# All three gate stages of a two-block kernel: pairs 2 to 17 by seven block products for eight on contraction tiles 0 to 3, in 256 columns

## The reference, cut to what matters

```python
D_MODEL, SEQ, D_FF = 1024, 512, 2816

def swiglu(x, w_gate, w_up, w_down):                     # stage gu0
    return (jax.nn.silu(x @ w_gate) * (x @ w_up)) @ w_down

def _conv_ffn(x, w_in, conv_w, conv_b, w_out):           # stages gu1, gu2
    s = x.shape[1]
    u = x @ w_in                                         # 1024 x 5632
    up = jnp.pad(u, ((0, 0), (CONV_WIDTH_2 - 1, 0), (0, 0)))
    u = sum(conv_w[j] * up[:, j:j + s] for j in range(CONV_WIDTH_2)) + conv_b
    g, val = u[..., :D_FF_2], u[..., D_FF_2:]
    return (jax.nn.silu(g) * val) @ w_out
```

## Time and profile before

| | |
|---|---|
| median of 3 runs | 1810.29 us (1809.44 to 1810.98) |
| the profiled execution, its own time | 1813.07 us |
| its span | 1811.3 us |
| mean granted clock of TensorE | 0.993 |
| busy: PE, DVE, ACT, POOL | 97%, 42%, 44%, 57% |
| the chain that ended last: PE, DVE, ACT | 84%, 10%, 2% |

### The profile page before, as it was taken

The page is one execution under the profiler, slowest core; times in us unless marked ns, Lnnn a source line. Parts: engine busy times, 40 slices in busy tenths (PEclk is TensorE's granted clock), DMA queues, the critical chain, the costliest instruction groups (busy, mean ns, idle before and its releaser), DMA issues.

```text
span 1811.3 us, 26859 instructions
## 1 busy us (share of the span) xinstructions
PE 1765.7 (97%) x8755; PEld 1478.9 (82%) x8755; DVE 768.1 (42%) x1382; ACT 796.2 (44%) x1674; POOL 1031.5 (57%) x926
## 2 busy tenths in 40 slices
PE   8999999999999999999999999989999999999997
PEld 6879888888887888798888888877777888888887
DVE  7973000001235556553333322487875533333224
ACT  5644332322245555464444422555555644444231
POOL 7956555555562333456666665555554666666651
PEclk9999999999999999989999999999999999999999
DMA  5212333333334454323333233333332233332332
GB/s 159 87 47 82 105 93 93 95 88 109 91 95 110 124 134 119 87 68 105 93 100 96 78 111 89 82 85 85 85 83 68 73 106 102 93 97 85 105 91 98
DMA packets 327252, 171.94 MB, mean 95 GB/s; under 512 B 43458, under 2 KB 316948, under 8 KB 327188
## 3 DMA queue, kind: packets, MB, share of 16 engines
q1 hardware_dynamic: 327172, 171.12, 33.6%
q10 hardware_dynamic: 16, 0.00, 0.0%
HBM read 152.15 MB, written 2.10 MB: 85 GB/s over the span
## 4 chain that ended last, share of the span: by engine, by line
PE 84%; DVE 10%; ACT 2%; issue 1%; DMA 1%; POOL 1%; SPq 1%; DVEq 0%; ACTq 0%
PE bank L983 23%; PE bank L985 23%; PE bank L984 23%; DVE score L2266 3%; PE attended L983 2%; PE attended L984 2%; PE attended L985 2%; PE turned L1424 1%; PE attended L1440 1%; PE bank L1056 1%; PE bank L1068 1%; DVE small L2454 1%; PE bank L1069 1%; ACT pmap L1861 1%; DMA raw<-in_a_w_in 0%
## 5 line engine op out<-in xcount | busy, mean ns | idle before, releaser
L742 POOL TENSOR_TENSOR WL<-raw,WH 128x512 fp32r<-128x512 f32 (+3 forms) x656 | 776.8, 1206 | 541.5 <-ACT WH L1605 538.9
L983 PE MATMUL bank<-XL,WH 128*128 128x512 f32 x1432 | 568.7, 397 | 3.7 <-DVE work L2577 1.2
L985 PE MATMUL bank<-XH,WL 128*128 128x512 f32 x1432 | 557.5, 389 | 0.0
L984 PE MATMUL bank<-XH,WH 128*128 128x512 f32 x1432 | 557.0, 389 | 0.0
L1605 ACT ACTIVATE WH<-raw 128x512 fp32r<-128x512 f32 (+3 forms) x656 | 338.4, 566 | 295.6 <-PE bank L985 183.2
L985 PEld LDWEIGHTS bank<-XH,WL 128*128 128x128 f32 x1432 | 269.3, 188 | 56.8
L983 PEld LDWEIGHTS bank<-XL,WH 128*128 128x128 f32 x1432 | 269.9, 188 | 55.6 <-DVE work L2577 1.5
L984 PEld LDWEIGHTS bank<-XH,WH 128*128 128x128 f32 x1432 | 270.1, 189 | 50.4
L983 PE MATMUL bank<-HL,WH 128*128 128x512 f32 (+1 forms) x528 | 198.6, 376 | 0.0
L985 PE MATMUL bank<-HH,WL 128*128 128x512 f32 (+1 forms) x528 | 198.4, 376 | 0.0
L984 PE MATMUL bank<-HH,WH 128*128 128x512 f32 (+1 forms) x528 | 198.4, 376 | 0.0
(11 more groups left out here) (366 smaller groups left out, 2534.0 us busy)
## 6 DMA issues: line engine op xcount, KB each, us to landing
raw<-in_ffn_w_in SPq DMA_DIRECT2D x88, 512.0 KB, 3.6
raw<-in_w_gate SPq DMA_DIRECT2D x22, 512.0 KB, 3.6
raw<-in_w_up SPq DMA_DIRECT2D x22, 512.0 KB, 3.7
raw<-in_ffn_w_out SPq DMA_DIRECT2D x28, 384.0 KB, 3.2
raw<-in_ffn_w_out SPq DMA_DIRECT2D x28, 320.0 KB, 3.2
raw<-in_a_w_in SPq DMA_DIRECT2D x16, 512.0 KB, 3.9
raw<-in_kv_w SPq DMA_DIRECT2D x32, 256.0 KB, 2.9
raw<-in_w_in SPq DMA_DIRECT2D x12, 512.0 KB, 3.6
```

Source lines behind the costliest of these rows:

```text
L742: pool.tensor_tensor(wl, x, wh, ALU.subtract).then_inc(w_lo, 1)
L983: pe.matmul(out_, wh, xl, start=start, stop=False)
L984: pe.matmul(out_, wh, xh, start=False, stop=False)
L985: return pe.matmul(out_, wl, xh, start=False, stop=stop)
```

## The change

Pairs 0, 1 and 18 to 21 stay as they were. For the 16 pairs 2 to 17 of each gate stage ("fast" pairs) the contraction tiles 0 to 3 are seen as a two by two block problem: two blocks of contraction tiles (0 and 1, 2 and 3), the two outputs (up, gate), two halves of 256 tokens. Seven block products stand for the eight, each of 2 contraction tiles, 3 matmuls, 256 columns (6 matmuls); contraction tiles 4 to 7 are multiplied plainly, in 256 columns too (48 matmuls). The output of a pair comes together in three PSUM banks of a set (two sets alternate); four intermediate sums are kept aside by ACT (`keep`), and DVE adds them to the finished halves (`pair_sum`), which gives the two banks `bank` that the rest of the pair reads as before.

The weights of a fast pair fall in three groups: **A**, plain weights of the first four contraction tiles (high and low of 6 tiles, 768 columns; raw buffer doubled), **S**, four sums of weights (8 tiles, 1024 columns; summed by DVE, high by ACT, low by DVE), and **P**, gate's and up's contraction tiles 4 to 7 (8 tiles, 1024 columns; high by ACT, low by POOL; one raw buffer, two sets of high and low). Four sums of tokens are made once a stage by DVE, split by ACT and DVE. The step names of PE's order are r1, a, q1, r2, u, r3, q, r. `clear_sums` moves from the norm ahead of the stage to behind the last fast pair. The core of the diff:

```diff
+FAST = ("gu0", "gu1", "gu2")
+FAST_FIRST, FAST_PAIRS = 2, 16
+FAST_LAST = FAST_FIRST + FAST_PAIRS - 1
+TAIL_PAIRS = range(FAST_LAST + 1, FT)
+FAST_STEPS = ("r1", "a", "q1", "r2", "u", "r3", "q", "r")
+KEPT = (("r1", 1.0), ("q1", -1.0), ("r2", -1.0), ("r3", -1.0))
+KEPT_OF_SUM = (0, 3, 2, 1)
+SUM_AFTER = ("u", "u", "q", "r")
+SETS_FREE = 2 * len(KEPT)
...
+def gu_items(name):
+    return 2 * (FT - FAST_PAIRS) if name in FAST else 2 * FT
...
+        raw_a = [raw_fast[:, :, :], raw[:, 0, :, :]]
+        raw_p = raw[:, 1, :, :]
...
+        WA = [ring_tiles(x, 0, 6) for x in (WH, WL)]
+        WS = [ring_tiles(x, 6, 8) for x in (WH, WL)]
+        WP = [[ring_tiles(x, 14 + 8 * b, 8) for x in (WH, WL)] for b in range(2)]
+        token_sums = [x[:, FAST_LAST + 1:FT, :] for x in (HH, HL)]
+        w_sums = work[:, 0:2, :].rearrange("p a (k n) -> p (a k) n", n=P)
+        kept_tiles = [work[:, 2 + 2 * b:4 + 2 * b, :].rearrange("p a (k s) -> p (a k) s", s=HALF) for b in range(2)]
...
+        fast_sets = [(sc[0], sc[1], tb[0]), (tb[1], ob[0], ob[1])]
...
+                def load_a(n, i):
+                    b = n.slot(2)
+                    for part, w, t in ((0, up, i + up_first), (4, gate, i)):
+                        sp.dma_start(raw_a[b][:, part:part + 4, :], w[:, 0:4, bass.ds(t.n() * P, P)]).then_inc(a_landed[b], 16)
+                def load_p(n, i):
+                    for part, w, t in ((0, gate, i), (4, up, i + up_first)):
+                        sp.dma_start(raw_p[:, part:part + 4, :], w[:, 4:DT, bass.ds(t.n() * P, P)]).then_inc(p_landed, 16)
+                def load_pair(i):
+                    n = fast_pair(name, i)
+                    sp.wait_ge(a_lo, n.n(-1))
+                    sp.wait_ge(w_summed, n.n(-1))
+                    load_a(n, i)
+                    sp.wait_ge(p_lo, n.n())
+                    load_p(n, i)
+                def load_plain(g):
...
+                def of_a(i):
+                    n = fast_pair(name, i)
+                    pool.wait_ge(a_hi, n.n(1))
+                    pool.tensor_tensor(WA[1], raw_a[n.slot(2)][:, 2:DT, :], WA[0].bitcast(F32), ALU.subtract).then_inc(a_lo, 1)
+                def of_p(i):
+                    n = fast_pair(name, i)
+                    b = n.slot(2)
+                    pool.wait_ge(p_hi, n.n(1))
+                    pool.tensor_tensor(WP[b][1], raw_p, WP[b][0].bitcast(F32), ALU.subtract).then_inc(p_lo, 1)
+                def of_hid(i):
+                    j = i.slot(2)
+                    pool.wait_ge(h_hi, (i + FT * layer).n(1))
+                    pool.tensor_tensor(HL[:, at(i), :], hid[:, j:j + 1, :], HH[:, at(i), :].bitcast(F32), ALU.subtract).then_inc(h_lo[j], 1)
+                def slot(i):
+                    of_a(i + 1)
+                    of_hid(i + -1)
+                    of_p(i + 1)
...
+                def add(out_, ws, xs, opens=False, closes=False):
+                    for t, (w, x) in enumerate(zip(ws, xs)):
+                        mm = product(out_, w[0], w[1], x[0], x[1], opens and t == 0, closes and t == 1, not opens)
+                    return mm
+                def plain(out_, side, c, ks=range(4)):
+                    for k in ks:
+                        w = [x[:, 4 * side + k, :] for x in WP[b]]
+                        mm = product(out_, w[0], w[1], XH[:, 4 + k, c], XL[:, 4 + k, c], False, k == 3, True)
+                    return mm
+                r, q = running[:, 0:HALF], second[:, 0:HALF]
+                u_gate, u_up = mixed[:, low_half], mixed[:, high_half]
+                x = (XH, XL)
+                pe.wait_ge(a_lo, n.n(1))
+                pe.wait_ge(pair_sums, n.times(4).n(4 + SETS_FREE - 8))
+                if b == 1:
+                    for side in range(2):
+                        pe.wait_ge(bank_read[side], STAGES[name][1] // 2 + 2)
+                add(r, weights(WA, 2), tokens(x, 0, low_half), True, True).then_inc(fast_mm, 1)
+                add(u_up, weights(WA, 0), sums_of_tokens(3), True, True)
+                add(u_gate, weights(WA, 4), tokens(x, 2, low_half)).then_inc(fast_mm, 1)
+                pe.wait_ge(p_lo, n.n(1))
+                plain(u_gate, 0, low_half, range(2))
+                plain(u_up, 1, low_half, range(2))
+                pe.wait_ge(s_lo, n.n(1))
+                add(q, weights(WS, 0), sums_of_tokens(1), True, True).then_inc(fast_mm, 1)
+                pe.wait_ge(kept, n.times(4).n(1))
+                add(r, weights(WS, 4), sums_of_tokens(2), closes=True).then_inc(fast_mm, 1)
+                plain(u_gate, 0, low_half, range(2, 4))
+                plain(u_up, 1, low_half, range(2, 4)).then_inc(fast_mm, 1)
+                pe.wait_ge(kept, n.times(4).n(3))
+                add(r, weights(WS, 2), sums_of_tokens(0), closes=True).then_inc(fast_mm, 1)
+                add(q, weights(WS, 6), tokens(x, 2, high_half))
+                plain(q, 0, high_half).then_inc(fast_mm, 1)
+                pe.wait_ge(kept, n.times(4).n(4))
+                plain(r, 1, high_half).then_inc(fast_mm, 1)
...
+            def keep(n, k):
+                step, sign = KEPT[k]
+                b = n.slot(2)
+                act.wait_ge(fast_mm, n.times(len(FAST_STEPS)).n(after(step)))
+                act.activation(kept_tiles[b][:, k, :], fast_sets[b][1 if step[0] == "q" else 2][:, 0:HALF], ACT.Copy,
+                               scale=sign).then_inc(kept, 1)
...
+            def a_high(name, i):
+                n = fast_pair(name, i)
+                b = n.slot(2)
+                act.wait_ge(a_landed[b], n.round(2, 1) * 32)
+                if first_fast(n):
+                    act.wait_ge(item_done, STAGES[name][0] + 2)
+                else:
+                    act.wait_ge(fast_mm, n.times(len(FAST_STEPS)).n(after("a") - len(FAST_STEPS)))
...
+            def p_high(name, i):
+                act.wait_ge(p_landed, n.times(32).n(32))
+                if isinstance(i.it, int) and i.base < FAST_FIRST + 2:
+                    act.wait_ge(item_done, STAGES[name][0] + 3 + b)
+                else:
+                    act.wait_ge(fast_mm, n.times(len(FAST_STEPS)).n(-len(FAST_STEPS)))
...
+            def s_high(name, i):
+                n = fast_pair(name, i)
+                act.wait_ge(w_summed, n.n(1))
+                if not first_fast(n):
+                    act.wait_ge(fast_mm, n.times(len(FAST_STEPS)).n(after("q") - len(FAST_STEPS)))
+                act.activation(WS[0], w_sums, ACT.Copy).then_inc(s_hi, 1)
...
+            def fast_gates(name):
...
+                def slot(i):
+                    n = fast_pair(name, i)
+                    keep(n, 0)
+                    hidden(i + -1)
+                    a_high(name, i + 1)
+                    p_high(name, i + 1)
+                    for k in range(1, 4):
+                        keep(n, k)
+                    s_high(name, i + 1)
...
+            def fast_conv_hidden(name, layer):
...
+                def slot(i):
+                    n = fast_pair(name, i)
+                    keep(n, 0)
+                    linear_fast(i + -1, 1)
+                    a_high(name, i + 1)
+                    p_high(name, i + 1)
+                    silu_fast(i + -1)
+                    keep(n, 1)
+                    keep(n, 2)
+                    hidden(i + -1)
+                    keep(n, 3)
+                    s_high(name, i + 1)
...
+                with act.Fori(0, FAST_PAIRS // 2 - 1) as it:
+                    for j in range(2):
+                        i = Nth(FAST_FIRST + 1 + j, it, 2)
+                        linear_fast(i + -1, 0)
+                        slot(i)
...
+            def sums_of_weights(name, i, m):
+                n = fast_pair(name, i)
+                b = n.slot(2)
+                dve.wait_ge(a_landed[b], n.round(2, 1) * 32)
+                if first_fast(n):
+                    dve.wait_ge(x_lo, DT + half_tile(m, 1, DT - 1) + 1)
+                else:
+                    dve.wait_ge(s_lo, n.n())
+                up, pairs = (raw_a[b][:, t:t + w, :] for t, w in ((0, 2), (2, 4)))
+                own.link(dve.tensor_tensor(w_sums[:, 0:4, :].rearrange("p (a k) n -> p a k n", a=2),
+                                           pairs.rearrange("p (a k) n -> p a k n", a=2),
+                                           up.unsqueeze(1).broadcast_to([P, 2, 2, P]), ALU.add))
+                own.link(dve.tensor_tensor(w_sums[:, 4:6, :], raw_a[b][:, 4:6, :], w_sums[:, 0:2, :], ALU.add))
+                dve.tensor_tensor(w_sums[:, 6:8, :], raw_a[b][:, 6:8, :], w_sums[:, 4:6, :], ALU.add).then_inc(w_summed, 1)
+            def sums_of_weights_low(name, i):
+                dve.wait_ge(s_hi, fast_pair(name, i).n(1))
+                dve.tensor_tensor(WS[1], w_sums, WS[0].bitcast(F32), ALU.subtract).then_inc(s_lo, 1)
+            def pair_sum(name, i, part):
+                n = fast_pair(name, i)
+                b = n.slot(2)
+                mixed, second, running = fast_sets[b]
```

(49 more changed lines are left out.)

357 lines of the change are left out of this document (346 added, 11 removed).

## The result

The changed kernel takes **1857.77 us** (median of three runs, 1855.35 to 1861.69), 1.0262 of the kernel before (95% interval 1.0247 to 1.0277): 47.5 us slower. The forecast was 1883, in a range of 1815 to 1935. The profiled execution took 1861.69 us with a span of 1859.9, 48.6 more than the span before.

A forecast was written before the change was run, and what follows sets the result against it. PE's streaming was taken to bound the kernel before, waits on the DVE-POOL lock to decide after: gu1 and gu2 +67.8, gu0 0, ends +4.8, together +72.6 on the median 1810.3, giving 1883 us, range 1815 to 1935.

The forecast's parts named there:

- The mechanism: gu1 and gu2: DVE's low of S and POOL's low of P shut each other out of SBUF for whole instructions.
- both orders: gu1, gu2: POOL's low of P first, next linear at 13.1 us; or DVE's low of S first, turns 14.3 then 11.2.
- the term "13.0": gu1 and gu2: 13.0 us a pair against 10.88 before, 32 pairs, +67.8 us.
- the price 0.120: PE in fast pairs: each 256-column product takes 0.120 us, so 90 take 10.80 us a pair against 10.88.
- a turn of 10.88: gu0: chain from low of S round to the next takes 10.88 us, equal to before; 16 pairs, 0 us.
- half width at half price: Rival, PE: half-width product takes 0.1133 us, 10.2 a pair, 32.6 us less, 1778 us; chance 0.01.
- the lock does not decide: Rival, gu1 and gu2: low of S never waits for POOL, 11.1 us a pair, 1822 us; chance 0.24.
- The clock: Rival, gu1: PE standstill lowers its clock, one pair in four at 19.2 us adds 50 us, 1933 us; chance 0.05.
- The ends: Each gate stage: 1.1 us behind the last fast pair, 0.5 at the head; 3 x 1.6 = 4.8 us.

## Why the prediction was right or wrong

- **The mechanism was right, for about half of the loss.** The prediction named the two instructions that meet, the place, both orders and what each makes late next (the low of S at once, or the next P by its one buffer). The orders were forecast at 13.1, and 14.3 with 11.2; they measured 12.7, and 13.8 with 11.0. With that meeting taken away, 0.75 of 1.6 us a pair came back. The working had P's one buffer as a cost of the second order alone; the run with the low of S from PSUM shows that it holds the pair up (11.71) where nothing of the lock delays S or P.
- **Its size in gu1 and gu2 was 0.5 us a pair too large**, 16.6 us in all: the term "13.0". The working runs true up to the low of A (ready at 2.55, released at 4.36; measured 2.53 and 4.39). It gave the three sums and the product until 6.90 and they were done at 6.46; the low of P was due at 9.0 and began at 8.69. The working was too slow on DVE in each link. The first sum ended 0.55 us after the release and not 0.69; the two linked sums began 0.03 us after the row ahead, where it had 0.14; and the product began 0.07 us before the row ahead ended, which the working allowed for ACT and not for DVE. It also took 13.0 for both orders, where its own 14.3 and 11.2 average 12.75; their measured mean is 12.4.
- **gu0 was a tie by the forecast, and gained 2.8 us.** The failed step is the price 0.120 taken from the earlier trace rows. It belongs to a place of the weights in SBUF and the new ring lies at another; the kernel's code has the 64 bytes and the working passed over them. The other half of that term, a turn of 10.88 with the low of P just clear of the low of S, was too long: PE's starts lose 1.25 us to waits in all 16 fast pairs.
- **The rival "half width at half price"** was given 0.01. Its price, 0.1133, is real for part of the time, and what it says of gu0 alone (10.2 a pair) was nearly reached with P's low short, 10.32. "TensorE: Matmul & The Clock Gate", section "Back-to-back issue gap", of the Trainium skill gives N/2.4 + 2.5 ns for an isolated matmul, by which 256 columns would take 109.2 ns, an estimate; the shortest steady distance in these runs is 0.1133 us. The rival could not have carried the kernel, with gu1 and gu2 held up by waits.
- **The rival "the lock does not decide"** was priced at 11.1 a pair and 1822 us. With seven of eight tiles of the low of P taken out, the run gave 11.15 and 1820. That the total agrees so well is partly luck: it holds some 9 us that gu0 gained by its price and the rival didn't have. With the full low of P and the low of S free, a pair took 11.7, so its chain lacks the way over P's buffer.
- **The clock** held: 0.994 over the execution. One stretch fell, after PE had waited 1.78 us in the first fast pair of gu1 for the first low of P: 16 products at half the full clock, 0.213 us apart, 1.6 us more than at full clock. gu2 waits as long at that place and keeps its clock, and its pairs are no shorter.

```profile
812.00:818.00 6.00, 3.72 (x27) 3.10 (x27) 5.64 (x6) 2.01 (x3) 6.00 (x3) 0.99 0.02 4
818.00:821.00 3.00, 3.00 (x16) 3.00 (x16) 0.00 (x0) 0.20 (x1) 0.84 (x1) 0.50 0.77 230
```

- **The ends** were right in sum: 4.8 forecast, 3 x 1.1 + 2 x 0.7 = 4.7 measured. A head of gu1 and gu2 costs 0.7 because PE waits 0.49 and 0.54 us, ahead of the first fast product, for DVE's low parts of the sums of tokens.

```profile
812.94 0.38 PE L1153 MATMUL turned<-XL,WH 128*128 128x256 f32 x1 [0.49 <-DVE HL L2923]
```

- The difference closes: 72.6 forecast less 48.6 measured is 24.0, of which 16.6 is the turn in gu1 and gu2, 3.8 gu0, 0.1 the ends, and 3.7 the stretch between gu0 and gu1 (24.2 in all).

## What to carry to other kernels

When an engine that isn't the bound takes over work with two SBUF operands, ask which POOL instruction will be running at that moment: the cost is up to the length of that instruction (2.25 us behind one of 2.40 here), and one exchange in the order was worth 21 or 25 us, another made it 13 worse, in ways that did not add up. Two things took the wait away here: an operand in PSUM, or a short instruction on POOL at the place where they meet. Then look at the buffer that this instruction gives back: with one buffer, its end, the next landing and all that stands behind it on ACT are one chain. And before paying for narrower matmuls, measure the product at the width and at the place in SBUF where its weights will lie: the 6% fewer columns were worth 0.24 us a pair of gu0 with one place and 0.04 with another.
